# One transformer layer on eight cores: the block kept feature-major, with pooling and merge matmuls between attention units

## What is computed

```python
mod_x = silu(c) @ mod_w + mod_b                 # shift, scale, gate for both sub-layers
hc = modulate(rms_norm(ctx, norm1_g), csh1, csc1)
kc = rms_norm(heads(hc @ Wk), k_norm_g);  vc = heads(hc @ Wv)
h = modulate(rms_norm(x, norm1_g), sh1, sc1)
q, k, v, pool_in, gate_logits = split(h @ w_in)
q = rope(rms_norm(q));  k = rope(rms_norm(k))
attn = window_attention(q, k, v, kc, vc, sink)  # blocks n-1, n, n+1 of 128, and all context keys
ga, gp = split(sigmoid(gate_logits + gate_b))
p = multiscale_pool(pool_in, pool_w, pool_scale) @ w_pool_proj   # windows 2, 4, 8, 16
mix = (ga * (attn @ w_attn_proj) + gp * p) @ w_out
x = x + g1 * mix
h2 = modulate(rms_norm(x, norm2_g), sh2, sc2)
a, b = split(h2 @ w_up)
x = x + g2 * ((silu(a) * b) @ w_down)
```

## Time and profile before

| | us |
|---|---|
| median of 3 runs | 1237.26 (1236.01 to 1238.42) |
| profiled execution, span of the slowest core | 1236.2 |
| spans of the 8 cores in it | 1220.1 to 1236.2 |
| TensorE busy | 1046.1 |
| VectorE busy | 582.1 |
| ScalarE busy | 459.0 |
| GpSimd busy | 218.2 |

### The profile page before, as it was taken

How to read it: one execution, slowest core, us unless ns; L and a number is a source line. 1 busy time by engine, 2 the same in 40 slices (tenths; PEclk the granted TensorE clock), 3 DMA queues, 4 the chain that set the end, 5 groups by cost and what they waited for, 6 DMA issues and landing times.

```text
span 1236.2 us, 15846 instructions; the slowest of 8 cores (1220.1 to 1236.2 us)
## 1 busy us (share of the span) xinstructions
PE 1046.1 (85%) x6092; PEld 504.1 (41%) x6182; DVE 582.1 (47%) x886; ACT 459.0 (37%) x696; POOL 218.2 (18%) x183
## 2 busy tenths in 40 slices
PE   2423699975888885599999998999999999999998
PEld 0112364332544442244444444444444444444443
DVE  1359738973667658333333287422235222442134
ACT  1238558984999943122222165211100111011100
POOL 2145324540000020011111056211100111001000
PEclk9755789987999997799999999899999999999999
DMA  9894020028445060435433193547400473013124
GB/s 159 150 251 143 1 35 1 1 40 123 65 65 87 2 61 0 69 31 51 38 30 30 39 250 71 52 42 99 40 1 6 45 95 34 1 18 36 17 102 170
DMA packets 108253, 78.78 MB, mean 64 GB/s; under 512 B 77842, under 2 KB 95506, under 8 KB 108050
## 3 DMA queue, kind: packets, MB, share of 16 engines
q0 software_dynamic: 97376, 43.88, 31.4%
q1 hardware_dynamic: 10802, 33.88, 8.3%
HBM read 113.24 MB, written 8.39 MB: 98 GB/s over the span
## 4 chain that ended last, share of the span: by engine, by line
PE 69%; issue 9%; ACT 9%; DMA 7%; DVE 5%; POOL 2%; ACTq 0%; POOLq 0%; SPq 0%; DVEq 0%
PE psall L919 25%; PE psall L814 14%; PE psall L943 12%; DMA mwr<-mod_w 5%; ACT pT L603 4%; PE psall L501 3%; PE psall L874 3%; PE psall L730 2%; PE psall L601 2%; PE psall L329 2%; PE psall L641 2%; PE psall L537 2%; DMA wo<-w_out 1%; DVE pT L608 1%; ACT sq L504 1%
## 5 line engine op out<-in xcount | busy, mean ns | idle before, releaser
L919 PE MATMUL psall<-h2T,wu 128*128 128x512 bf16 x1379 | 305.0, 381 | 1.7 <-issue 0.2
L919 PEld LDWEIGHTS psall<-h2T,wu 128*128 128x128 bf16 x1408 | 138.2, 98 | 167.8 <-issue 3.0
L922 ACT ACTIVATE sil<-psall 128x512 f32<-128x512 f32 x88 | 52.5, 597 | 352.6 <-PE psall L919 346.3
L923 DVE TENSOR_TENSOR actT<-psall,sil 128x512 bf16<-128x512 f32 x88 | 60.5, 690 | 221.4 <-PE psall L919 221.4
L603 ACT ACTIVATE pT<-psall 128x1024 bf16<-128x1024 f32 x160 | 148.0, 1036 | 24.1 <-PE psall L601 21.8
L943 PE MATMUL psall<-wd,actT 128*128 128x512 bf16 x690 | 151.7, 379 | 0.7
L946 DVE TENSOR_TENSOR xacc<-xacc,psall 128x512 f32<-128x512 f32 x96 | 66.0, 687 | 86.0 <-PE psall L943 86.0
L943 PEld LDWEIGHTS psall<-wd,actT 128*128 128x128 bf16 x704 | 68.8, 98 | 83.2
L231 POOL DMA_DIRECT2D wu<-w_up x44 | 38.6, 878 | 332.1 <-PE psall L919 327.9
L329 PE MATMUL psall<-mwr,clhs 128*128 128x512 bf16 x119 | 35.3, 454 | 49.8 <-DMA mwr<-mod_w 47.8
L501 PE MATMUL psall<-hT,wring 128*128 128x512 bf16 (+1 forms) x327 | 75.5, 375 | 1.3 <-DVE kcT L488 0.6
(11 more groups left out here) (136 smaller groups left out, 1337.7 us busy)
## 6 DMA issues: line engine op xcount, KB each, us to landing
mwr<-mod_w POOLq DMA_DIRECT2D x12, 1024.0 KB, 16.1
wu<-w_up POOLq DMA_DIRECT2D x44, 256.0 KB, 5.4
xblk<-xext SPq DMA_DIRECT2D x18, 512.0 KB, 9.7
xacc<-xext SPq DMA_DIRECT2D x16, 512.0 KB, 25.1
out<-xacc SPq DMA_DIRECT2D x16, 512.0 KB, 2.6
wd<-w_down POOLq DMA_DIRECT2D x2, 1792.0 KB, 16.8
mbr<-modb_rep SPq DMA_DIRECT2D x12, 256.0 KB, 5.6
ropet<-rope_cs SPq DMA_DIRECT2D x1, 2304.0 KB, 20.6
```

The source lines that it names most:

```text
L919: T.op("pe", lambda e, k=k, ab=ab: e.matmul(ps[bs + ab][:], lhsT=wu[us][:, ab, k, :], rhs=h2T[:, k, cc * 512:(cc + 1) * 512], start=(k == ...
L923: T.op("dve", lambda e: e.tensor_tensor(out=actT[:, fi, cc * 512:(cc + 1) * 512], in0=ps[bs + 1][:], in1=sl[:], op=ALU.mult), reads=[PS(bs ...
```

## The change

The whole block is rewritten. The main parts:

- x, ctx and the output are laid out feature-major by the host, and weights in the order in which tiles read them. The norm is made on `[feature, token]` tiles: squares (`sq`), a matmul with ones for the sum over features (`mm`), Ln and Exp (`root`), a product (`hat`), and scale and shift as columns (`mod`). The transposes go away.
- Modulation for the first norm comes as columns: `mod_w` is loaded in fp32 by SP (`m1f`), cast, and multiplied with a two-column right side. The other four parts (`dot`) are products along rows on VectorE, each with its own 512 KB load into the single buffer `stg`.
- Projection goes chunk by chunk (k, v, k, v, 8 q), with the norm of the next chunk spread between its units. The sum of the rotary parts moves from VectorE to GpSimd.
- Attention units are recorded with four fillers each. Units 0 to 7 take the pooling projection, its sums (now on GpSimd, `pl_chain`), and the product of pool_w with w_pool. Units 8 to 31 take the merge of chunks 0 to 2 (`c1_groups`), one tile each, and one `dot`. The gate is a tanh instead of a sigmoid. The merge of chunk 3 follows attention, behind dot(24) to dot(31).
- Output projection, second norm and FFN are feature-major. g1 and g2 are columns in the final product, so the products into wo and wd go away.
- There are no barriers: a tile that lies on older ones waits for their readers and writers alone (`olds`).

Cut to what is spoken of:

```diff
@@ Trk
+    def tile(self, off, shape, dtype, name):
...
+        self.olds[name] = [n for (n, o, z) in self.tiles if o < off + size and off < o + z]
...
-    def barrier(self, skip=()):
...
@@ build_program: norm, modulation
+        def hat(k):
+            T.op("dve", lambda e: e.tensor_tensor(out=src[:, k, :], in0=src[:, k, :], in1=rs[:, :n], op=ALU.mult),
+                 reads=[(sk, "x"), ("rs",)], writes=[(sk, "h", k)])
+        def mod(k):
+            T.op("dve", lambda e: e.tensor_scalar(out=dst(k), in0=src[:, k, :], scalar1=modab[:, k, 1, var:var + 1],
+                                                  scalar2=modab[:, k, 0, var:var + 1], op0=ALU.mult, op1=ALU.add),
...
+    for fb in range(4):
+        mod_block(fb)
+    load_rope(0)
+    for k in range(8):
+        n0[3](k)
+    dma("sp", xst[2][:], ctxd.rearrange("p (k n) -> p k n", k=8), ("xst2", "x"), "xst2")
+    for fb in range(8):
+        mod_cols(fb)
+        if fb + 4 < 8:
+            mod_block(fb + 4)
+        if fb == 2:
+            load_x(1, 1)
+            load_rope(1)
+        n0[4](fb)
+    dma("pool", wq[1][:], kview(wqd[1]), ("wq1",), "wq1")
@@ qk_tail
-                T.op("dve", lambda e: e.tensor_tensor(out=sc["t1"][:, :n], in0=sc["t1"][:, :n], in1=sc["t2"][:, :n], op=ALU.add),
+            T.op("pool", lambda e: e.tensor_tensor(out=sc["t1"][:, :n], in0=sc["t1"][:, :n], in1=sc["t2"][:, :n], op=ALU.add),
...
@@ spread_norm
+        for k in range(8):
+            put(k // 2, lambda k=k: sq(k))
+            put(k // 2 + 1, lambda k=k: mm(k))
+            put(6 + k // 2, lambda k=k: (hat(k), mod(k)))
+        put(5, root)
@@ pl_chain
+        for lv in range(gi + 1):
...
+            T.op("pool", lambda e, nx=nx, cur=cur, lo=lo, d=d: e.tensor_tensor(
+                out=nx[:, lo:LU], in0=cur[:, lo:LU], in1=cur[:, lo - d:LU - d], op=ALU.add), reads=ck, writes=nk)
+            cur, ck = nx, nk
+        T.op("dve", lambda e: e.tensor_tensor(out=cur[:, wo_:wo_ + 8], in0=cur[:, wo_:wo_ + 8], in1=pedg[:, 2 + gi * 8:10 + gi * 8], op=ALU.mult),
...
+    plf = [lambda: pl_proj(0, 0), lambda: pl_proj(0, 1), lambda: pl_proj(0, 2), lambda: (pl_proj(0, 3), pl_halo(0), pl_chain(0)),
...
+    plf += [pl_scale]
+    for g in range(4):
+        plf += [lambda g=g: pl_comp(g, 0), lambda g=g: pl_comp(g, 1)]
@@ c1_groups, dot
+        def g_p():
+            mm(b1, lambda k: cw[:, 1, k, :], hr, hk, [wk], 8)
+            T.op("act", lambda e: e.activation(out=gp[:], in_=ps[b1], func=AF.Tanh, bias=gbh[:, 8 + j:9 + j], scale=0.5),
...
+    def dot(i):
+        dma("sp", stg[:], mod2d[i], ("stg",), "stg")
+        T.op("dve", lambda e: e.scalar_tensor_tensor(out=stg[:], in0=stg[:], scalar=1.0, in1=crep[:], op0=ALU.mult, op1=ALU.mult,
+                                                     accum_out=dotc[:, i // 8, i % 8:i % 8 + 1]),
@@ attention
-        sfn[0](); pvc[0](); sfn[1](); prev_tail(); pvc[1](); sfn[2](); pvc[2](); sfn[3](); pvc[3](); sfn[4]()
-        if ui % 4 == 1 and ui // 4 < 8:
-            mod_chunk(4 + ui // 4, False, mwr2, mbr2, clhs2, ("clhs2",), bankbase=7)
+        if ui < 8:
+            f = plf[4 * ui:4 * ui + 4]
+        elif ui < 32:
+            f = c1_groups(ui % 8, ui // 8 - 1, (6, 7, 6, 7))
+        s[0](); f[0](); s[1](); p0(); f[1](); s[2](); p1(); f[2](); s[3](); ptail(); f[3](); s[4]()
+        if 8 <= ui < 32:
+            dot(ui - 8)
...
+    load_xacc(0)
+    for i in range(24, 32):
+        dot(i)
+    dot_fin(3)
+    for j in range(8):
+        for g in c1_groups(j, 3, (4 * (j % 2), 4 * (j % 2) + 1, 4 * (j % 2) + 2, 4 * (j % 2) + 3)):
+            g()
+        if j in (1, 4, 6):
+            load_xacc({1: 1, 4: 2, 6: 3}[j])
@@ second norm
+        eng = "dve" if k % 2 == 0 else "pool"
+        T.op(eng, lambda e: e.tensor_tensor(out=tmp[ti][:], in0=xacc[cc][:, k, :], in1=r[:], op=ALU.mult),
...
@@ FFN
+    for p in range(3):
+        f0, nf = FPASS[p]
+        if p > 0:
+            for fi in range(nf):
+                load_wu(f0 + fi)
+                for cc in range(4):
+                    d1_unit(f0 + fi, fi, cc)
+        for cc in range(4):
+            for j in range(8):
+                d2_unit(p, cc, j, p == 2)
+        if p == 0:
+            load_wd(2)
```

More of the change, by code:

```diff
@@ L58, in op @@
         for k in reads:
-            st = self._st(k)
+            st = self._st(k, add)
             if st["w"] is not None:
@@ new lines, in load_m1 @@
+    def load_m1(fb):
+        i = fb % 4
+        dma("sp", m1f[i][:].rearrange("p a b c -> p (a b c)"), mod1d[fb], ("m1f%d" % i,), "m1f%d" % i)
+    dma("sp", fcon[:], fcond, ("fcon",), "fcon")
+    load_x(0, 0)
+    for fb in range(4):
+        load_m1(fb)
+    dma("pool", cmt[:], cmat, ("cmt",), "cmt")
+    dma("pool", wkv[:], kview(wkvd), ("wkv",), "wkv")
+    dma("pool", wq[0][:], kview(wqd[0]), ("wq0",), "wq0")
+    T.op("dve", lambda e: e.memset(ones[:], 1.0), writes=[("ones",)])
+    T.op("act", lambda e: e.activation(out=csil[:], in_=cTf.rearrange("p (v k) -> p k v", v=2), func=AF.Silu),
+         reads=[("fcon",)], writes=[("csil",)])
@@ new lines, in v_unit, with vc_unit, spread_norm, put @@
+    def v_unit(ci, h):
+        t0 = CH[ci][0] + h * 256
+        v_pair(hT, lambda j: ("hT", ci, j), t0, Vaug, t0 // 128, ("Vaug", t0 // 256))
+    def vc_unit():
+        v_pair(hcT, lambda j: ("hcT", j), 0, Vcaug, 0, ("Vcaug", 0))
+    def spread_norm(nm):
+        sq, mm, root, hat, mod = nm
+        sl = {}
+        def put(i, f):
+            sl.setdefault(i, []).append(f)
+        for k in range(8):
+            put(k // 2, lambda k=k: sq(k))
+            put(k // 2 + 1, lambda k=k: mm(k))
+            put(6 + k // 2, lambda k=k: (hat(k), mod(k)))
+        put(5, root)
+        return sl
@@ new lines, in build_program @@
+    k_unit(4, 0)
+    v_unit(4, 0)
+    k_unit(4, 1)
+    kc_unit(0)
+    vc_unit()
+    kc_unit(1)
+    qk_tail()
+    NPP = 8
+    pT = [T.tile(kb(95.75 + 2 * i), [128, 2, 512], BF16, "pT%d" % i) for i in range(NPP)]
+    Otok = [T.tile(kb(111.75 + i), [128, 4, 2, 64], BF16, "Otok%d" % i) for i in range(2)]
+    wpl = T.tile(kb(185.75), [128, 8, 512], BF16, "wpl")
+    wps = T.tile(kb(193.75), [128, 4, D], BF16, "wps")
+    pwf = T.tile(kb(201.75), [128, 4, 128], F32, "pwf")
+    pwb = T.tile(kb(203.75), [128, 4, 128], BF16, "pwb")
@@ L577, in b_scores, with s_pair @@
         slots = []
-        qk = [[("qT", 4 * jj + r, n) for r in range(4)] for hf in range(2)]
-        def s_pair(ki, kind, kb):
+        def s_pair(ki, kind, kbk):
             sp = bctr["s"] % 2
@@ new lines, in build_program @@
+    late = []
+    for cc in range(4):
+        for j in range(8):
+            c2_unit(cc, j, (cc * 8 + j) % 6)
+            for f in late[:2]:
+                f()
+            late = late[2:]
+            if j >= 2:
+                ss_mm(cc, j - 2)
+        if cc == 0:
+            for f in range(3):
+                load_wu(f)
+        if cc < 3:
+            late += [lambda cc=cc: ss_mm(cc, 6), lambda cc=cc: (ss_mm(cc, 7), n2_root(cc))] + \
+                    [(lambda cc=cc, k=k: n2_mod(cc, k)) for k in range(8)]
@@ new lines, in build_program @@
+    order = [(f, cc) for f in range(3) for cc in range(3)] + [(f, 3) for f in range(3)] + [(f, cc) for f in range(3, 8) for cc in range(4)]
+    tails = [lambda: ss_mm(3, 6), lambda: (ss_mm(3, 7), n2_root(3))] + [(lambda k=k: n2_mod(3, k)) for k in range(8)]
+    for f in late:
+        f()
+    for i, (f, cc) in enumerate(order):
+        if f >= 3 and cc == 0:
+            load_wu(f)
+        d1_unit(f, f, cc)
+        if i == 0:
+            for t in tails:
+                t()
+            wd[1] = T.tile(kb(171.25), [128, 8, D], BF16, "wd1")
+            load_wd(1)
```

1339 lines of the change are left out of this document (584 added, 755 removed).

## The result

| | before | after |
|---|---|---|
| median of the runs | 1237.7 us | 1271.3 us (1270.8 to 1272.5) |
| span of the profiled execution | 1236.2 us | 1269.4 us |
| TensorE busy | 1046.1 us, 85% | 1024.3 us, 81% |

A forecast was written before the change was run, and what follows sets the result against it. TensorE, busy 85%, was the bound, its idle time before 523 us. 1236 - 22 (start, projection) + 28 (attention, merge) - 8 (second norm) + 21 (FFN) = 1255 us; own range 1215 to 1295, overall 1190 to 1305.

The forecast's parts named there:

- units 0 to 7: Attention units carrying pooling: wait for wpl 8 us, unit 0, chains, then units 5 to 7 at 17; 117 us together.
- pooling chains: Units 1 to 4: masks and Otok queue on VectorE behind GpSimd's sums; 13.6, 18, 23 us from chain to chain.
- the dots: Last merge quarter: dot(24) to dot(31) each wait for a load into stg, 54 us; TensorE stalls 38 us.
- wd(2): FFN after the first down pass: its load holds up wu in GpSimd's queue; 22 us wait, 1 to full clock.
- ptail wait: Units 8 to 31: ptail on TensorE waits for the second Otok triple, 0.9 us more, 10.45 us a unit.
- The order of the two DMA queues at the start: Start: GpSimd's queue runs ahead, 3.2 MB in 28 us, SP's 13.6 MB takes 41; with 5 to begin, 74 us.
- a few restarts at half clock: 5: Attention with fillers: TensorE restarting at half clock a few times, 5 us in all.
- The estimate of 4.9 us: Projection: a unit with hats and mods, VectorE taking turns with GpSimd; 4.9 us, between 4.3 and 5.8.
- (1): Projection: VectorE and GpSimd take no turns, ScalarE sets the chunk at 30 us; 1211 us total, chance 0.27.
- (2): Projection: TensorE loses its clock, 27 us a chunk become 55 at half speed; 1311 us total, chance 0.07.
- (3): Attention: tanh and exponential need different tables, 4 reloads a unit on ScalarE; 1322 us total, chance 0.05.
- (4): Attention: fillers do not fill, 10.65 us a unit; 1260 us total, inside the forecast's range, no separate chance.

The follow-up runs named there:

- Experiments 1 to 3: Changed kernel, separately: dots behind their merge tiles (1.012; 0.998 with x loads moved too), wd(2) issued mid second up pass (1.010), VectorE's pooling-chain part one unit later (1.010).
- e6_rs_psum: Changed kernel with the first norm's inverse root written to PSUM instead of SBUF, so the hat has one SBUF input: 1257.9 us, ratio 1.016.
- experiment 5: Changed kernel with inverse root in PSUM (1257.9 us) or rotary sum back on VectorE (1265.4 us); kernel before with that sum on GpSimd (1241.3 us).
- e4_ptail: Changed kernel with ptail (a unit's transposes) behind the fourth filler, except in units 8, 16 and 24: 1253.2 us, ratio 1.013.

## Why the prediction was right in its direction and short in its size

| term | predicted | measured | |
|---|---|---|---|
| dense projection starts | 74 | 63.4 | -11 |
| three chunks | 41, 41, 41 | 45.4, 41.8, 41.6 | +6 |
| last chunk, halo, ctx | 49 | 56.8 | +8 |
| units 0 to 7 | 117 | 122 | +5 |
| units 8 to 31, last one, restarts | 258 | 256 | -2 |
| last merge quarter | 87 | 92 | +5 |
| second norm | 65 | 67 | +2 |
| FFN to the end | 482 | 483 | +1 |
| span | 1255 | 1269.4 | +14 |

**Direction.** Right, and for the stated reasons. The three new waits were each named, placed and priced: pooling chains (13.6, 18, 23 against 13.4, 17.9, 21.2 from chain to chain), the dots (54 us against 53, with a gap of 38 against 36.0), wd(2) (22 + 1 against 19.5 and a restart). Experiments 1 to 3 show each as a cause: take it out, and the time falls by about its price. The ptail wait of 0.9 us a unit measured 1.0, the unit 10.42 against 10.45. For the chains the close agreement is in part luck: a sum was priced at 4.6 us and took 3.6, while the transposes, the projection and the halo behind it were priced at 2.7 and took 4.1 to 4.9.

**Size.** The forecast excess of 18 us was a small difference of large terms, -22 + 28 - 8 + 21, and the terms are short by 14 together, so the loss came out at 33.5 us. One overlap was wrong, and the rest was mis-sized:
- *The order of the two DMA queues at the start* is the step that was wrong in kind. The prediction let GpSimd's queue run ahead, with both wq landed by 28 us, and x behind it. It didn't run ahead. The times from issue to landing of the two wq loads, issued at 3.1 and 4.0 us, and TensorE at the second (start, us):

```profile
DMA to landing us min/median/max: 66.9/74.4/81.9
...
85.98 3.60 PE L397 MATMUL psall<-hT,wq 128*128 128x512 bf16 x8 [6.17 <-DMA wq<-w_q]
```

  They landed at 70 and 86 us, while SP's loads went on beside them: in the first 64 us the hardware queue moved 15.0 MB in 71.7% of the engines' time and the software queue 2.18 MB in 26.6%. So x landed at 61.6, not 74, with a megabyte of weights still to come, and the start came 11 us earlier; the first chunk paid for it with a wait of 6.2 us for wq and a granted clock of 0.84, and took 45.4 us instead of 41.
- *The projection from its dense start on*, 172 predicted, 186 measured, is the largest mis-sized term; the start hid most of it. Besides the first chunk it is the end, 56.8 instead of 49 (43 + 10 - 4 in the prediction, where no row stood for the 10). There VectorE has the hats and mods of two small norms, busy for 9.6 of 10 us from 202 and for 12.4 of 12.7 from 225.5, and TensorE waits 9.7 us for its products. Six of the sixteen mods of 256 columns took 1.24 us beside GpSimd where the others took 0.41, 5 us in all. From 238.3 to 248.8 GpSimd's sums and products (1.27 us each) follow one another and set the pace.
- *Units 0 to 7*, 117 predicted, 122 measured. Units 5 to 7: 17 us predicted, some 21.4 measured (the ptails start at 347.89 and 369.28, three units). I took ScalarE's exponentials as the pace, with some copies; in the chain of waits exponential, mask, Otok, ptail and the next score pair follow one after another, since little filler stands between, and at the granted clock of 0.76 some score pairs take 0.61 us instead of 0.39. The wait for wpl was 10.6 instead of 8. The fourth chain's sums took 15.6 us instead of 18.4, which gave some back.
- *The last quarter and the second norm*, 5 and 2 us. The gap ended 56 us into the quarter, not 54, and the 152 matmuls behind it took 35.7, not 32.8 (152 x 0.216).

The common cause of the last points is that I priced work behind a wait at its steady pace. The term "a few restarts at half clock: 5" covered attention alone; the two stretches with the most waits have a granted clock of 0.76 in the table above, and a row of before had shown the like, 0.51 at 57 to 135. How much of the 14 us the restarts carry is argued from these clocks; no experiment separates it.

Two sums of the prediction don't come out of their own terms, and neither matters here. Its bounds, taken as independent, give 1222 to 1279 and not 1215 to 1295. And from the end of g_p to the second Otok its terms make 3.1 us, not 3.3, so 0.8 a unit and not 0.9; 0.95 was measured in most units.

**The estimate of 4.9 us** for a unit with hats and mods was low: 5.57. Mod takes its turn with GpSimd (1.37 against 0.55), which the prediction had left between 4.3 and 5.8. The second and third chunk came out at 41.8 and 41.6 all the same, since their other units took 41.8 - 4 x 5.57 = 19.5 us where the prediction had 21.4: right as a sum, not in its parts. The Trainium skill (SBUF, State Buffer, "Who interferes with whom") says of VectorE operations with two SBUF inputs, and of two-port modes, which a tensor_scalar can enter, that they contend with GpSimd; the trace agrees, with mod at 1.37 and, in e6_rs_psum, a hat freed of its second SBUF input at 0.67. By the page the prediction had put a chunk nearer 45; it was 41.7 for the reason above.

**The rivals.** (1) No turns, 1211: false, by experiment 5. With the hats' turns gone the gain is 13 us, not the 44 of the rival. Part of the rest are mod's turns, which no edit took out; but where nothing waits, VectorE's operations of such a unit start every 0.66 us (two products), 0.71 (hat) and 0.46 (mod), 3.7 us in all, and that is more than ScalarE's 2.4. So these units could not have come down to ScalarE's pace, which the rival needs. (2) Clock lost in the projection, 1311: 0.84 to 0.96 in its chunks, not 0.5. (3) Table reloads, 1322: two loads in all the attention, at L546 and L751, 1.28 us each; the Trainium skill (ScalarE: Activation LUTs, "Table sets: the hidden batching unit") has exponential and tanh in one set, and the trace agrees. (4) Fillers that don't fill, 10.65 a unit: 10.42 measured, and 9.41 in e4_ptail, so they fill, but for the wait of ptail.

**The tests named in the prediction.** First projection at about 62 and dense at 74: a first one at 48.4 and dense at 63.4. 41 us a chunk: 45.4, 41.8 and 41.6. Hats ending 0.5 behind GpSimd: 0.56. Attention at 246: 249. Waits for VectorE up to 20 us in units 1 to 4: 17.5 and 9.2 the longest. A 38 us gap, released by VectorE waiting for stg: 36.0. 22 us for wu and no other in FFN: 19.5, and none over 1 us.
